# The half-rotation of rotary embedding, from four ScalarE copies to one permutation matmul on TensorE

## The reference

```
def rope(x, pos):
    half = x.shape[-1] // 2
    ...
    x1, x2 = xf[..., :half], xf[..., half:]
    return concatenate([x1 * cos - x2 * sin, x2 * cos + x1 * sin], axis=-1)
```

## Time and profile before

| | us |
|---|---|
| median of 3 executions | 1370.9 |
| lowest, highest | 1368.59, 1372.19 |
| the profiled execution: its own time | 1372.19 |
| its span, first to last instruction | 1370.3 |
| PE busy | 1341.7 (98% of the span) |
| DVE busy | 876.7 (64%) |
| ACT busy | 598.0 (44%) |
| mean granted TensorE clock | 0.992 of full |

### The profile page before, as it was taken

One profiled execution on the slowest core, in us unless ns is written; L12 is line 12 of the kernel. 1 busy time (PEld: TensorE's weight loads), 2 busy tenths in 40 slices (PEclk: granted clock), 3 DMA queues, 4 the chain that ended last, 5 costly groups with the idle time before them and its releaser, 6 DMA issues.

```text
span 1370.3 us, 25666 instructions
## 1 busy us (share of the span) xinstructions
PE 1341.7 (98%) x10999; PEld 1296.7 (95%) x10999; DVE 876.7 (64%) x1616; ACT 598.0 (44%) x1064; POOL 33.1 (2%) x57
## 2 busy tenths in 40 slices
PE   7999999999999999999999979999999999999998
PEld 6999978999999999999999956999999999999998
DVE  5535677587777776322886689578777777522386
ACT  4222245554444443222755667546444444322372
POOL 2000100000000000000010010000000000000000
PEclk9999999999999999999999989999999999999999
DMA  8321641312223323322423320221233223322231
GB/s 258 111 91 55 216 148 62 93 47 65 91 93 93 93 93 123 106 86 79 139 64 123 93 71 15 78 93 47 83 90 93 91 93 94 128 90 101 64 134 63
DMA packets 34498, 131.85 MB, mean 96 GB/s; under 512 B 4212, under 2 KB 4684, under 8 KB 34112
## 3 DMA queue, kind: packets, MB, share of 16 engines
q1 hardware_dynamic: 29520, 112.42, 25.6%
q0 software_dynamic: 4864, 17.78, 4.0%
HBM read 121.54 MB, written 10.05 MB: 96 GB/s over the span
## 4 chain that ended last, share of the span: by engine, by line
PE 87%; DVE 8%; ACT 3%; DMA 1%; issue 1%; SPq 0%; DVEq 0%; ACTq 0%
PE tile L955 22%; PE tile L959 22%; PE tile L957 22%; PE tile L965 4%; PE tile L966 4%; PE tile L967 4%; DVE wL L1490 1%; DMA raw<-in_w_kv 1%; DVE sm L2112 1%; DVE cv L1515 1%; PE side L1410 1%; PE sums L1428 1%; ACT wH L548 1%; DVE cg L1495 1%; DVE soft L2127 1%
## 5 line engine op out<-in xcount | busy, mean ns | idle before, releaser
L955 PE MATMUL tile<-xH,wH 128*128 128x260 f32 x1840 | 374.8, 285 | 12.5 <-DVE xL L1574 8.5
L548 ACT ACTIVATE wH<-raw 128x1024 fp32r<-128x1024 f32 (+1 forms) x192 | 212.9, 1111 | 384.0 <-DMA raw<-in_w_up 145.2
L959 PE MATMUL tile<-xH,wL 128*128 128x260 f32 x1840 | 372.2, 284 | 0.0
L957 PE MATMUL tile<-xL,wH 128*128 128x260 f32 x1840 | 371.7, 284 | 0.0
L1490 DVE TENSOR_TENSOR wL<-raw,wH 128x1024 fp32r<-128x1024 f32 (+1 forms) x192 | 247.9, 1291 | 149.0 <-ACT wH L548 144.7
L955 PEld LDWEIGHTS tile<-xH,wH 128*128 128x128 f32 x1840 | 285.1, 190 | 16.9 <-issue 12.7
L959 PEld LDWEIGHTS tile<-xH,wL 128*128 128x128 f32 x1840 | 285.2, 189 | 0.0
L957 PEld LDWEIGHTS tile<-xL,wH 128*128 128x128 f32 x1840 | 284.7, 189 | 0.0
L1530 DVE TENSOR_TENSOR u<-tile,rstd 128x520 f32<-128x520 f32 x96 | 67.2, 700 | 138.1 <-PE tile L959 138.1
L955 PE MATMUL tile<-hidH,wH 128*128 128x260 f32 x616 | 124.2, 283 | 0.0
L959 PE MATMUL tile<-hidH,wL 128*128 128x260 f32 x616 | 123.8, 282 | 0.0
(11 more groups left out here) (364 smaller groups left out, 1874.8 us busy)
## 6 DMA issues: line engine op xcount, KB each, us to landing
raw<-in_w_up SPq DMA_DIRECT2D x88, 512.0 KB, 3.6
raw<-in_w_down SPq DMA_DIRECT2D x32, 704.0 KB, 4.0
raw<-in_w_ple SPq DMA_DIRECT2D x16, 512.0 KB, 5.4
raw<-in_w_kv SPq DMA_DIRECT2D x12, 512.0 KB, 3.8
raw<-in_w_qo SPq DMA_DIRECT2D x12, 512.0 KB, 3.6
raw<-in_w_qkv SPq DMA_DIRECT2D x12, 512.0 KB, 3.6
cring<-in_c_in POOLq DMA_DIRECT2D x8, 512.0 KB, 4.4
out_c_s<-cring POOLq DMA_DIRECT2D x8, 512.0 KB, 3.1
```

What stands on the lines that cost most here:

```text
L548: nc.scalar.activation(wH[j][:, 0:n], raw[j][:, 0:n], ACT.Copy).then_inc(s_high, 1)
L955: nc.tensor.matmul(out[:, q, 0:HT], wh, x[0][:, k, tokens(q)], start=first, stop=False)
L957: nc.tensor.matmul(out[:, q, 0:HT], wh, x[1][:, k, tokens(q)], start=False, stop=False)
L959: mm = nc.tensor.matmul(out[:, q, 0:HT], wl, x[0][:, k, tokens(q)], start=False, stop=last)
```

## The change

`rotate` moves from ACT to PE. It becomes two matmuls (one for each token half) of a 128x128 permutation matrix with `u`, both plain float32, into the PSUM tile `side`. They are issued behind chunk c for tile c - 1, from c = 3 on; the last, for tile 11, stands between the scores of group 0 and those of group 1. They wait for the read of their tile and, since `side` has room for one, for rope's multiply of the tile before. DVE's multiply by the sine reads `side` in PSUM in place of `rotated` in SBUF. The permutation matrix adds 128 columns to the constants. On DVE, shift(1) moves from ahead of rope(11) to behind it. The arithmetic is the same.

```diff
-C_IDENT, C_ONES, C_CAUSAL, C_BAND = 0, P, 2 * P, 3 * P
-C_SEL = 5 * P
+C_IDENT, C_ONES, C_CAUSAL, C_PERM, C_BAND = 0, P, 2 * P, 3 * P, 4 * P
+C_SEL = 6 * P
...
-            def rotate(t):
-
-                act.wait_ge(s_read, READ0["qkv"] + t + 1)
-                if t > 3:
-                    act.wait_ge(s_rotr, t - 3)
-                half = HD // 2
-                for i in range(P // half):
-                    last = nc.scalar.activation(rotated[half * i:half * i + half, t % 2, :],
-                                                u[half * (i ^ 1):half * (i ^ 1) + half, t % 2, 0:T], ACT.Copy)
-                last.then_inc(s_rot, 1)
-
             for c in range(COUNT["qkv"]):
                 high(*ahead("qkv", c + 2))
-                if c >= 2:
-                    rotate(c)
...
+            def rotate(t):
+
+                pe.wait_ge(s_read, READ0["qkv"] + t + 1)
+                if t == 2:
+                    pe.wait_ge(s_vtr, 2)
+                if t > 2:
+                    pe.wait_ge(s_rotr, t - 2)
+                for q in range(2):
+                    mm = nc.tensor.matmul(side[:, q, 0:HT], perm, u[:, t % 2, tokens(q)],
+                                          start=True, stop=True)
+                mm.then_inc(s_rot, 1)
+
...
                 if c == 2:
                     turn_values()
+                if c >= 3:
+                    rotate(c - 1)
...
             window_scores(0)
+            rotate(COUNT["qkv"] - 1)
             window_scores(1)
...
-                nc.vector.tensor_tensor(cv[:], rotated[:, t % 2, :], sin_t[:], ALU.mult).then_inc(s_rotr, 1)
+                nc.vector.tensor_tensor(halves(cv[:]), side[:, :, 0:HT], halves(sin_t[:]), ALU.mult).then_inc(s_rotr, 1)
...
             shift(0)
-            shift(1)
             rope(COUNT["qkv"] - 1)
             for gi in range(groups):
-                if 0 < gi < groups - 1:
+                if gi + 1 < groups:
                     shift(gi + 1)
```

More of the change, by code:

```diff
@@ L187, in build @@
         causal = const[:, C_CAUSAL:C_CAUSAL + P]
+        perm = const[:, C_PERM:C_PERM + P]
         band = const[:, C_BAND:C_BAND + 2 * P]
@@ L202, in build @@
         y_down = at("y_down", [P, KT, T], xL_at)
-        rotated = at("rotated", [P, 2, T], xL_at)
         ff = Region(arena)
@@ L2207, in _constants @@
     c[:, C_CAUSAL:C_CAUSAL + P] = np.where(r[None, :] >= r[:, None], 0.0, NEG)
+    c[r, C_PERM + (r ^ (HD // 2))] = 1.0
     c[:, C_BAND:C_BAND + P] = np.where(r[None, :] >= r[:, None], 0.0, NEG)
```

## The result

The changed kernel takes 1377.55 us in the median (1376.25 to 1378.79, 6 runs) against 1370.39 us (1368.59 to 1372.45, 6 runs): +7.2 us, a ratio of 1.0051 with a 95% interval of 1.0039 to 1.0062 (5.3 to 8.5 us). Forecast were 1378.2 us and +7.3 us. The profiled execution has a span of 1376.9 us against 1370.3 before.

What follows compares the result with a forecast made beforehand. PE was taken to bound the projection stage, DVE to be the fuller engine in the attention loop. 7.04 + 0.2 + 0 + 0.1 = 7.3 us on the median 1370.9 gave 1378.2 us, range 1374.7 to 1381.

Steps and rivals of the forecast that it cites:

- The bound of the stage: Projection stage: PE alone bounds it, 5.77 us per chunk, growing to 6.65; time freed on ACT is worth 0.
- The price of one rotation: Projection stage: one f32 matmul pair costs PE 0.88 us, so eight between chunks 3 to 11 add 7.04 us.
- The rotation of tile 10: Behind chunk 11: rope(10) on DVE now waits for this rotation on PE, +0.2 us.
- The rotation of tile 11 and the swap: Attention loop's start: rotation ready before rope(11) asks; DVE does the same work in another order without a gap, 0 us.
- The narrow margin: Attention loop's start: group 1's exponentials end near 803.3, just before DVE asks for them, some 0.6 us to spare.
- The constants: Program's start: the second DMA of constants grows by 64 KB, +0.1 us, between zero and 1.3 us.
- The clock: Attention loop's start: PE's clock still falls, some 3 us later, and stays low as long; shift(4) starts as before, 0 us.
- the case with a falling clock: Attention loop: slow period at 802 to 812 us, group 4's scores end about 810 as before; the forecast, chance 0.58.
- Rival (a): Loop's start: clock stays at 2.4 GHz, group 4's shift at 808.5 instead of 810.0, sum 5.6, 1376.5 us; chance 0.25.
- One test of the prediction: Loop's start on DVE: normalise(0) starting more than half a microsecond off 801.5 + 7 would make the prediction wrong.
- Rival (b): Loop's start: ACT's last rotation and table load set the pace; their relief gives 1372.2 us, not slower; chance 0.07.
- Rival (c): Projection stage: each rotation costs its whole 1.04 us, without overlap or waiting for DVE; 9.2 in all, 1380.1 us; chance 0.10.

Runs made afterwards that it cites:

- double: The changed kernel with each rotation of tiles 2 to 9 issued twice in a row; median 1385.01 us, ratio 1.0114 to the kernel before.
- half: The changed kernel with only the first token half rotated for tiles 2 to 9; median 1375.58 us, ratio 1.0042 to the kernel before.
- cheaper: The changed kernel with the f32 matmuls of tiles 2 to 9 replaced by same-size rounded-float32 ones on other data; ratio 1.0015 to the kernel before.
- busy matmuls: Unread f32 matmuls put into PE's waits at the loop's start: changed kernel 1376.64 us, kernel before 1369.95, kernel before with only the last rotation on TensorE 1368.84.

## Why the prediction was right

**The bound of the stage** was read rightly: step 6.62 us against a forecast of 6.65, no idle of PE at the boundaries, and relief on ScalarE worth nothing (shown by leaving three quarters of it out).

**The price of one rotation** was taken from a row of the same shape elsewhere in the program, 0.88 us, and measured 0.85 by the step. Eight made 6.8 us in place of 7.04. It lies between the bounds of 0.48 and 1.04.

**The rotation of tile 10**: +0.2 us, measured 0.23 at rope(10) and 0.20 at normalise(0). It is in the forecast's sum, while the forecast's paragraph on the clock lets shift(4) start where it did, behind slow scores that would swallow it. The two do not go together. What is left at shift(4) is best seen in the traces whose clock stayed up: 13.85 and 13.87 us behind the read of chunk 11 with the change's order in the loop, 13.75 and 13.76 without it, so 0.1 us. The 0.19 us of the two main traces holds another 0.1 us from their differing falls of the clock.

**The rotation of tile 11 and the swap**: 0, and nothing showed for either alone. The narrow margin, the exponentials of group 1, held as reckoned: they end at 809.59 and normalise(1) starts at 810.27, 0.7 us later (0.6 forecast). The first exponential came 0.6 us earlier, not 0.8.

**The constants**: +0.1 us was put down. No run shows it; PE's wait for weights between 24 and 60 us was 1.6 us in the changed kernel (1.9 before) and 0.2 to 2.2 us in the experiments, so anything of this size is lost there.

**The clock**: the case with a falling clock came true in the profiled execution, from 809.0 us, which is 802 without the shift of 7 us, inside the 800 to 806 of the forecast. It rose after 6.8 us, a little sooner than the 7 to 10 said. The case that was built on the removal of the long idle stretch did not come: the clock fell with stretches of 0.69, 1.37 and 1.42 us. That the wait for the scores of group 4 stayed what it was, 1.99 against 1.91 us, is in part luck. The fall was shorter than forecast, and in the other traces with a fall this wait is anything from 0.50 to 2.02 us. The weight of 0.58 to 0.25 between the two cases fits what the traces show: of the four with the changed kernel's order in the loop and no busy matmuls (changed, double, half, cheaper) the clock fell in three. It is a chance of the single execution, though, and not a property of the kernel, so a part of the 1.5 us, by that weight some 0.4 us, could have gone into the expected time. **Rival (a)**, the steady clock, had its size right: it put shift(4) 808.5 - 794.64 = 13.86 us behind the read, and 13.85 and 13.87 were measured where the clock stayed up.

**One test of the prediction failed as it was worded**: normalise(0) was to start within half a microsecond of 801.5 + 7. It started at 807.88, 0.6 us early, because this execution was 0.43 us early at the first chunk and the eight rotations cost 0.2 us less. Measured from the read of chunk 11 it stood at 6.85 us, where 6.86 was forecast. A position in a trace should be forecast from the last fixed point ahead of it.

**The chances**, as listed, add up to 0.58 + 0.10 + 0.9 x 0.25 = 0.905 for slower and not to 0.88; nothing hangs on the difference.

The account closes: 6.82 us in the stage (801.03 - 741.23 against 794.64 - 741.66, chunk 2's read to chunk 11's), 0.19 us to shift(4), and 0.43 us the other way before the stage, make 6.6, the difference of the spans. From chunk 2's read to shift(4) the changed kernel's trace thus loses 6.82 + 0.19 = 7.0 us.

**Rival (b)**, not slower because the chain of waits ran over ScalarE there, is refuted by the last rotation alone on TensorE. **Rival (c)** is refuted by the step and by the second rotation costing no more than the first.

## What to carry to other kernels

Work moved off an engine that nobody waits for is worth nothing, and put onto the engine that bounds the stage it costs its full stream time, here eight times 0.85 us, even if it is neat there. Before moving a data movement to TensorE, look for the stretches where TensorE waits: one of the ten rotations had such a place, and that one cost nothing, but nobody needed it. The price of a matmul that the trace already has elsewhere in the same type and shape is a good price; read it to the second instruction behind it, as the first one starts before the cost has shown.

## What the runs showed of the hardware

A pair of plain float32 matmuls of 128x128 by 128x260 takes 0.85 to 0.88 us of TensorE's stream, a pair of the same shape in the rounded float32 type (on other data) 0.22 us by the step and 0.24 by the rows, in the same place and with the same waits. The next matmul after a float32 one starts early (0.68 us behind the pair's start) and the one after that is late.

The granted clock can fall during PE's waits at the loop's start or not fall, with the same instructions there: it was at 1.2 GHz for about 10 us in one execution, for 6.8 us in others, and not at all in the one of the cheaper matmuls. What that costs depends on whether the slow stretch meets scores that VectorE waits for, between 0 (it ended before them) and 1.7 us.

It can fall with PE busy throughout. Behind very narrow matmuls at about 102 us it was low for 3.4 or 6.8 us in all twelve traces, and behind the 32 matmuls of 128x8 at about 877 us for 0, 3.4 or 6.8 us. At 102 us the longer stretch cost 1.6 us more. In the runs this goes with the time: beside the last experiments, the fifteen runs of the kernel before with a mean granted clock of 0.992 average 1371.3 us, the four with 0.996 average 1366.2 us.
